# The front of a two-block layer on one core: first weight unit with the first 512 tokens, state-space set-up between low parts, rotations on GpSimd

## The reference

```python
h = rmsnorm(x, g_pre_mix)
proj = jnp.einsum('bld,dn->bln', h, w_in)
(u_s5, x_conv, b_conv, c_conv, q, k, v, f_logit, gate_logits) = jnp.split(proj, offsets, axis=-1)
y_a = s5_mixer(u_s5, a_re, a_im, log_dt, b_re, b_im, c_re, c_im, d_skip, w_glu)
y_b = short_conv_mixer(x_conv, b_conv, c_conv, conv_w)
```

## Time and profile before

| | |
|---|---|
| median of 3 runs | 3327.33 (3326.53 to 3329.29) |
| profiled execution, own time | 3331.32 |
| its span from first to last instruction | 3329.5 |
| mean granted TensorE clock | 0.997 |
| PE busy | 3262.3 (98%) |
| DVE busy | 1937.3 (58%) |
| ACT busy | 1278.2 (38%) |
| POOL busy | 1168.2 (35%) |

### The profile page before, as it was taken

How to read it: one execution, slowest core, us unless ns; L and a number is a source line. 1 busy time by engine, 2 the same in 40 slices (tenths; PEclk the granted TensorE clock), 3 DMA queues, 4 the chain that set the end, 5 groups by cost and what they waited for, 6 DMA issues and landing times.

```text
span 3329.5 us, 41035 instructions
## 1 busy us (share of the span) xinstructions
PE 3262.3 (98%) x16387; PEld 2695.8 (81%) x16387; DVE 1937.3 (58%) x2749; ACT 1278.2 (38%) x2023; POOL 1168.2 (35%) x487
## 2 busy tenths in 40 slices
PE   7899999999999999999999999999999999999998
PEld 6788877888888888788878888888888888888787
DVE  6874446543547766777643344445744376666676
ACT  4223444443136454534533333333332253233433
POOL 2443101444422444455112222222443145455453
PEclk9999999999999999999999999999999999999999
DMA  4233102234533444643421212213335232333553
GB/s 131 64 78 109 32 20 77 101 114 171 180 124 114 164 161 160 213 162 120 139 92 51 63 49 64 63 56 99 111 123 193 98 114 101 114 114 114 196 165 132
DMA packets 242713, 378.75 MB, mean 114 GB/s; under 512 B 22184, under 2 KB 180564, under 8 KB 229852
## 3 DMA queue, kind: packets, MB, share of 16 engines
q1 hardware_dynamic: 212140, 255.58, 24.2%
q10 hardware_dynamic: 26000, 109.81, 8.4%
q0 software_dynamic: 4384, 10.74, 0.9%
HBM read 263.66 MB, written 110.33 MB: 112 GB/s over the span
## 4 chain that ended last, share of the span: by engine, by line
PE 90%; DVE 4%; ACT 2%; DMA 2%; issue 1%; POOL 1%; SPq 0%; ACTq 0%; DVEq 0%; POOLq 0%
PE ps L1327 27%; PE ps L351 17%; PE ps L2201 13%; PE ps L842 5%; PE ps L306 3%; PE ps L1482 2%; PE ps L1484 2%; PE ps L1473 2%; PE ps L327 2%; PE ps L334 2%; PE ps L333 2%; PE ps L3871 2%; PE ps L3842 1%; PE ps L368 1%; PE ps L2243 1%; PE ps L3350 1%
## 5 line engine op out<-in xcount | busy, mean ns | idle before, releaser
L298 POOL TENSOR_TENSOR wlo<-raw,whi 128x2048 fp32r<-128x2048 f32 (+1 forms) x85 | 296.9, 3493 | 874.3 <-ACT whi L290 873.9
L1327 PE MATMUL ps<-h_hi,own 128*128 128x512 f32 x1200 | 385.5, 389 | 0.0
L1327 PE MATMUL ps<-tb,whi 128*128 128x512 f32 x1200 | 369.5, 389 | 0.0
L351 PE MATMUL ps<-h_lo,whi 128*128 128x512 f32 x880 | 352.3, 400 | 4.6 <-POOL wlo L298 4.6
L351 PE MATMUL ps<-h_hi,wlo 128*128 128x512 f32 x880 | 344.8, 392 | 0.0
L997 POOL TENSOR_TENSOR own<-raw,own 128x1024 fp32r<-128x1024 f32 x50 | 139.7, 2794 | 423.8 <-ACT own L987 423.8
L1025 POOL TENSOR_TENSOR wlo<-wsum,whi 128x2048 fp32r<-128x2048 f32 x50 | 239.4, 4788 | 100.5 <-ACT whi L1020 100.5
L1327 PEld LDWEIGHTS ps<-tb,whi 128*128 128x128 f32 x1200 | 225.2, 188 | 47.2 <-POOL wlo L1025 0.4
L1327 PEld LDWEIGHTS ps<-h_hi,own 128*128 128x128 f32 x1200 | 225.3, 188 | 46.5
L2201 PE MATMUL ps<-dw,h_lo 128*128 128x512 f32 x1104 | 253.3, 389 | 0.0
L2201 PEld LDWEIGHTS ps<-dw,h_lo 128*128 128x128 f32 x1104 | 207.3, 188 | 43.0
(11 more groups left out here) (424 smaller groups left out, 7325.8 us busy)
## 6 DMA issues: line engine op xcount, KB each, us to landing
raw<-in_w_in_dram SPq DMA_DIRECT2D x57, 512.0 KB, 4.4
raw<-in_w_in_dram SPq DMA_DIRECT2D x28, 1024.0 KB, 5.3
f_keep<-fr ACTq DMA_DIRECT2D x27, 1024.0 KB, 3.9
raw<-in_w_ff_dram SPq DMA_DIRECT2D x24, 1024.0 KB, 5.7
s_keep<-fr ACTq DMA_DIRECT2D x24, 1024.0 KB, 5.2
xh<-s_keep SPq DMA_DIRECT2D x48, 512.0 KB, 3.7
g_keep<-fr ACTq DMA_DIRECT2D x20, 1024.0 KB, 3.9
fr<-g_keep SPq DMA_DIRECT2D x20, 1024.0 KB, 5.0
```

The source lines that it names most:

```text
L298: nc.gpsimd.tensor_tensor(wlo[c % 2][:, 0:cols], raw[c % 2][:, 0:cols], whi[c % 2][:, 0:cols].bitcast(F32), ALU.subtract).then_inc(s_lo.se ...
L351: x = nc.tensor.matmul(ps[:, bank, :], w(a, k, m * P, P), H[b][:, k, sl], start=j == 0, stop=j == 23)
L1327: last = nc.tensor.matmul(ps[:, bank, :], w[p][:, k, :], x[r][:, k, :], start=k == 0 and q == 0, stop=k == 3 and q == 2)
```

## The change

- `Start`: the x pairs 2 and 3 are issued behind the square of tile 2. ScalarE makes the high part of unit 0 ahead of the h_hi parts, and each tile's square stands behind two h_hi parts. VectorE has `step_argument` ahead of the first h_lo, and the other pieces of the set-up (step size, decay argument, angle, reduction) between the h_lo parts of tokens 512 to 1023; ScalarE has the two tanh and two sine functions there.
- SP: unit 0 waits for x pair 0 instead of 1, unit 1 for x pair 2 instead of unit 0.
- TensorE: only blocks 0 and 1 are turned before the low part of unit 0 is waited for; block k + 2 is turned behind pass k; blocks of tokens 512 to 1023 are turned with unit 1.
- GpSimd: `turns` (45 tensor_tensor ops of 32 columns) and `first_tables` (24 ops of 32 to 256 columns) are new on it and gone from VectorE; VectorE waits for them ahead of `turn_tables(0)`. In group 1 the low part of (1,1) comes ahead of the half tables.
- VectorE, group 0: `first_half` follows `turn_tables`; `inputs` and then both `by_c` follow `powers`.
- TensorE: 14 half tiles instead of 16 lie ahead of the outputs of group 0; of the two others one comes before and one behind `turn_y(0)`.
- ScalarE, group 1: the high part and `x_tile(1,0)` come ahead of gelu.

```diff
@@ Start.act
-                e.wait_ge(x_pair[0].sem, 16)
-                load(2)
-                load(3)
-                for t in range(8):
+                for t in range(4):
                     r.act_pre(e, t)
-                    if t == 3:
-                        e.wait_ge(dv.sem, self.d + 1)
-                    if t == 5:
-                        split_hi(e, unit_no(0))
+                    if t == 2:
+                        load(2)
+                        load(3)
+                e.wait_ge(dv.sem, self.d + 1)
+                split_hi(e, unit_no(0))
+                for t in range(4, 8):
                     if t == 7:
                         split_hi(e, unit_no(1))
-                    if t >= 4:
-                        r.act_hi(e, 0, 2 * t - 8)
-                        r.act_hi(e, 0, 2 * t - 7)
+                    r.act_hi(e, 0, 2 * t - 8)
+                    r.act_hi(e, 0, 2 * t - 7)
+                    r.act_pre(e, t)
+                self.parameters.function(e, 0)
                 for k in range(8):
                     r.act_hi(e, 1, k)
+                    if k == 3:
+                        self.parameters.function(e, 1)
+                for n in (2, 3):
+                    self.parameters.function(e, n)
@@ Start.dve
+                p = self.parameters
+                p.step_argument(e)
+                for t in range(4, 8):
+                    r.dve_lo(e, 0, 2 * t - 8)
+                    r.dve_lo(e, 0, 2 * t - 7)
+                    r.dve_norm(e, t)
                 for k in range(8):
                     r.dve_lo(e, 1, k)
+                    if k == 0:
+                        p.step_size(e)
+                    elif k == 1:
+                        p.decay_argument(e)
+                    elif k == 2:
+                        p.angle(e)
+                    elif k in (3, 4, 5):
+                        p.reduced(e, k - 3)
+                    elif k == 6:
+                        p.angle_argument(e)
@@ S5AndConv.sp
-                e.wait_ge(x_pair[1].sem, 16)
+                e.wait_ge(x_pair[0].sem, 16)
...
                     if j == 0:
-                        e.wait_ge(ld[0].sem, 16)
+                        e.wait_ge(x_pair[2].sem, 16)
@@ S5AndConv.act
                 for f in range(4):
-                    if f:
+                    if f == 1:
+                        split(f, 1)
+                        x_tile(f, 0)
                         gelu(f - 1)
...
@@ S5AndConv.pool
+                def turns():
+
+                    S = [sm[:, j, :] for j in range(20)]
+                    e.wait_ge(m["s5_cos"], 1)
+                    r, i = S[8], S[7]
+                    for k in range(3):
+                        tt(S[18], r, i, ALU.mult)
+                        tt(MR[:, 0, :], r, r, ALU.mult)
+                        tt(MI[:, 0, :], i, i, ALU.mult)
+                        tt(MR[:, 0, :], MR[:, 0, :], MI[:, 0, :], ALU.subtract)
+                        tt(MI[:, 0, :], S[18], S[18], ALU.add)
+                        r, i = MR[:, 0, :], MI[:, 0, :]
+                    for j in range(6):
...
+                def first_tables():
...
+                turns()
                 split(0, 0)
+                first_tables()
                 for f in range(4):
-                    if f < 2:
-                        if f:
-                            half_tables(f)
-                        split(f, 1)
-                    else:
-                        split(f, 1)
+                    split(f, 1)
+                    if f:
                         half_tables(f)
@@ S5AndConv.dve
                     if f == 0:
-                        first_tables()
+                        e.wait_ge(m["s5_turns"], 1)
+                        e.wait_ge(m["s5_first"], 1)
                         turn_tables(f)
-                        by_c(f, 0)
+                        first_half()
                     powers(f)
...
                     else:
+                        inputs(f)
+                        by_c(f, 0)
                         by_c(f, 1)
-                        first_half()
                         taps(f)
                         by_b(f, 0)
                         kernel_rows(f)
                         by_b(f, 1)
-                        inputs(f)
@@ S5AndConv.pe
-                for k in range(KT):
-                    r.turn(e, 0, k)
+                r.turn(e, 0, 0)
+                r.turn(e, 0, 1)
                 lo_w(0)
                 for k in range(KT):
-                    r.turn(e, 1, k)
                     e.wait_ge(lo_made.sem, r.lo + k + 1)
                     u_passes(0, 0, k, 0)
+                    if k + 2 < KT:
+                        r.turn(e, 0, k + 2)
                 lo_w(1)
                 for k in range(KT):
+                    r.turn(e, 1, k)
                     u_passes(1, 0, k, 2)
...
-                    half_tiles((2, 0, 3, 3)[f])
+                    half_tiles((2, 1, 3, 3)[f])
                     if f:
                         turn_y(f - 1)
-                    if f > 1:
+                    if f:
                         half_tiles(1)
...
-                    half_tiles(6 if f else 7)
+                    half_tiles(6 if f else 5)
                     outputs(f)
```

More of the change, by code:

```diff
@@ L670, in hybrid_kernel, with __init__, link, tt @@
         m = {n: x.sem for n, x in m.items()}
+        class Parameters:
+            def __init__(self):
+                self.n = 0
+                self.S = [sm[:, j, :] for j in range(20)]
+            def link(self, e, ins):
+                ins.then_inc(m["s5_step"], 1)
+                self.n += 1
+                e.wait_ge(m["s5_step"], self.n)
+            def tt(self, e, o, a, b, op):
+                self.link(e, nc.vector.tensor_tensor(o, a, b, op))
+            def ts(self, e, o, a, s1, op0, s2=None, op1=ALU.bypass):
+                self.link(e, nc.vector.tensor_scalar(o, a, s1, s2, op0, op1))
+            def function(self, e, n):
+                o, i, fn, sc = ((1, 0, ACT.Tanh, 0.5), (5, 4, ACT.Tanh, 0.5), (7, 6, ACT.Sin, 1.0), (8, 6, ACT.Sin, 0.5))[n]
+                if n != 3:
+                    e.wait_ge(m["s5_arg"], n + 1)
+                nc.scalar.activation(sm[:, o, :], sm[:, i, :], fn, scale=sc).then_inc(m["s5_fun"], 1)
+            def expm1(self, e, o, th):
+                S = self.S
+                self.ts(e, S[10], th, -1.0, ALU.mult, 1.0, ALU.add)
+                self.link(e, nc.vector.reciprocal(S[10], S[10]))
+                self.tt(e, o, th, S[10], ALU.mult)
+                self.ts(e, o, o, 2.0, ALU.mult)
+            def step_argument(self, e):
+                S = self.S
+                e.wait_ge(m["s5_ld"], 16 * 5)
+                e.wait_ge(m["s5_d"], 16)
+                self.ts(e, S[9], S[19], 1.4426950408889634, ALU.mult)
+                self.ts(e, S[9], S[9], MAGIC, ALU.add, -MAGIC, ALU.add)
+                self.ts(e, S[9], S[9], -127.0, ALU.max, 127.0, ALU.min)
+                self.ts(e, S[0], S[9], -LN2_PARTS[0], ALU.mult)
+                self.tt(e, S[0], S[0], S[19], ALU.add)
+                self.ts(e, S[10], S[9], -LN2_PARTS[1], ALU.mult)
+                nc.vector.tensor_tensor(S[0], S[0], S[10], ALU.add).then_inc(m["s5_arg"], 1)
+                self.ts(e, S[9], S[9], 127.0, ALU.add, 8388608.0, ALU.mult)
+                self.link(e, nc.vector.tensor_copy(ki[:, :], S[9]))
+            def step_size(self, e):
+                S = self.S
+                e.wait_ge(m["s5_fun"], 1)
+                self.expm1(e, S[2], S[1])
+            def decay_argument(self, e):
+                S = self.S
+                self.ts(e, S[2], S[2], 1.0, ALU.add)
+                self.tt(e, S[2], S[2], ki[:, :].bitcast(F32), ALU.mult)
+                nc.vector.tensor_tensor(S[4], S[3], S[2], ALU.mult).then_inc(m["s5_arg"], 1)
+            def angle(self, e):
+                S = self.S
+                self.tt(e, S[6], S[11], S[2], ALU.mult)
+                self.ts(e, S[9], S[6], 1.0 / TWO_PI, ALU.mult)
+                self.ts(e, S[9], S[9], MAGIC, ALU.add, -MAGIC, ALU.add)
+            def reduced(self, e, *parts):
+                S = self.S
+                for c in parts:
+                    self.ts(e, S[10], S[9], -PI_PARTS[c], ALU.mult)
+                    self.tt(e, S[6], S[6], S[10], ALU.add)
+            def angle_argument(self, e):
+                S = self.S
+                self.ts(e, S[6], S[6], 3.1415925, ALU.min, -3.1415925, ALU.max)
+                nc.vector.tensor_copy(S[12], S[6]).then_inc(m["s5_arg"], 1)
@@ L2478, in act @@
                             e.wait_ge(d_u[q].sem, 16)
-                    x_tile(f, 0)
+                    if f != 1:
+                        x_tile(f, 0)
                     if f:
@@ L2590, in dve @@
[L2590 to L2600, removed]
@@ L4074, in hybrid_kernel @@
         start = add(Start())
-        mixers = add(S5AndConv(start.rows))
+        mixers = add(S5AndConv(start.rows, start.parameters))
         mixers.decay = add(Decay())
```

118 lines of the change are left out of this document (44 added, 74 removed), and 2 rows, old and new, of the table m.

## The result

The changed kernel took **3335.59 us** (median of 11 runs, 3332.93 to 3338.95), the kernel before 3327.8 beside it on the same chip: ratio 1.0023, interval 1.0016 to 1.0031. It is slower by a little more than the 0.2% that can be told from no change. The forecast was 3326.5 in a range up to 3335: wrong by 9.1 us, and on the side that the sum had left to a rival.

A forecast was written before the change was run, and what follows sets the result against it. TensorE was taken as the bound, with some 11.4 us of waits and 2.4 of slow matmuls to win. Outputs +3.8 and group 1's front -4.6 gave -0.8: 3330.5 profiled, scaled to a 3326.5 median, range 3317 to 3335.

The forecast's parts named there:

- Part 4: GpSimd's turns and first tables: turn ops 0.29 each, 13.1 us in all; tables ready at 91.2, VectorE waits 8.4.
- Part 6: Path to group 0's output products: kernel rows at 125.1, state products 2.7, outputs at 137.6, 3.8 later than before.
- Part 7: Front of group 1: 7.6 us of waits and 2.4 of slow matmuls go, 5.4 of work comes, 4.6 gained.
- Parts 1 to 5: From first weight load to half tile 8: early first pass, late last turn and tables, TensorE standing 6.8 us.
- Part 2: TensorE's passes with turns among them: last turn at 57.2, u products end at 80.4 against 78.26, early start spent.
- Part 1: First weight unit, loaded behind x pair 0: first pass at 24.6, 5.4 us sooner than before.
- Lock per op: Rival: each turn op alternates with a VectorE op, 0.45 apiece; outputs at 146.3, total 3335; chance 0.14.
- Part 4 and 5: GpSimd tables, then VectorE's order behind them: two low parts block 2.2 each, by_c ends at 113.7, TensorE stands 6.8.
- Tables in time: Rival: GpSimd's tables are ready when VectorE finishes WT (82.8); 9.4 us gained, total 3318; chance 0.30.
- The load is no sooner: Rival: first weights share with x pair 1, land near 19, all up to 4 us later; 3330; chance 0.06.

The follow-up runs named there:

- b_group1: Kernel before with only the group 1 edits: half tiles moved, low part of (1,1) ahead of the half tables, x_tile(1,0) ahead of gelu; 3329.82 us, ratio 1.0006.
- o_pool: Changed kernel with only its front undone (weights behind x pair 1, all turns ahead as before); 3324.31 us, ratio 0.9987.
- a_low: Changed kernel, with GpSimd's low part of conv unit (1,1) held back until the states of group 0 are done; 3334.73 us, ratio 1.0021.
- b_front: Kernel before with the new front alone (early weights, turns between passes), set-up and tables left in VectorE's list; 3339.3 us, ratio 1.0032.
- o_tables_low: Changed kernel with the old front, first tables back on VectorE, and low part of (1,1) held until the states are done; 3322.09 us, ratio 0.9982.
- a_tiles: Changed kernel with the half tiles back where they were, GpSimd order kept; 3335.59 us, ratio 1.0021.
- o_low_tiles: o_tables_low with the half tiles also back where they were before the change; 3320.27 us, ratio 0.9975.

## Why the prediction was wrong

**Where it failed.** Three steps: the price of the turn ops in Part 4 (1.4 us by the time the tables are there), the state products of Part 6 (2.0), and the gain of Part 7 (2.6 of 4.6 not there). The last two both belong to the edits at the front of group 1: forecast at 4.6 faster, they came out 1.9 slower (not told apart from no change) when tested alone in b_group1, and that is the larger half of the miss.

**What held.** The mechanism of Parts 1 to 5 is in the trace: the early first pass, the last turn late, the set-up free between low parts, the tables late, VectorE waiting on them, TensorE standing at half tile 8 (5.7 and, new, 2.9 before it, where 6.8 was forecast), two half tiles fewer before the outputs. Part 2 said that the early start is spent, and o_pool against the changed kernel shows it with 11.3 us.

**Part 1 and 2, too late by 2.** The first pass came at 22.4, not 24.6; the last turn ended near 54.8, not 57.2; the u products ended level with before (conv tile read at 83.9 against 84.0), not 2.1 later. It is one error carried through: ScalarE began the high part at 14.16 where the estimate was 15.9. It was on the safe side and should have made the result better.

**Part 4, the first step that failed.** A turn op was priced at 0.29; 38 of the 45 came every 0.33, and the last seven every 0.7 to 0.8, the last lasting 1.3, each held by a VectorE op of 512 or 1024 columns (BA and WT had started, which the step had left out for the turns, though it charged it for the tables). 57.98 to 76.4 is 18.4 us instead of 13.1 to 13.5. That ate the 2.5 which the turns began early and 2.4 more. It is the rival "Lock per op" in part: it decided from 0.43 apiece, and the mean was 18.4 / 45 = 0.41. The low part behind the turns then waited for the VectorE product that had begun 0.18 before it, and took 3.31 where the step had 2.4: it ended at 79.8, forecast 76.4. The tables won 2.0 of this back, 12.8 instead of 14.8, by luck: only the first of their ops was caught (0.98), where the step had charged the first eight with 3.6. So they were there at 92.6, forecast 91.2. The step's own terms are added up 0.8 too high (60.5 + 13.1 is 73.6, not 74.0, and 76.4 + 10.8 + 3.6 is 90.8, not 91.2), which hid as much of the miss.

**Part 4 and 5, a queue not looked at.** The low part of conv unit 1 moved behind the tables on GpSimd. The step charged what it blocks on VectorE (rightly: 4.1 for the two), but not that TensorE waits for it: 2.9 at 95.1, with a slower clock behind it (0.91). It probably cost little of its own, as TensorE stood later for the C product anyway; no run tests that.

**Part 6.** 137.6 was forecast, 141.5 measured. kernel_rows ended at 127.1, not 125.1: 1.4 from the tables, the rest in small pieces behind them. The other 2.0 is the low part of unit (1,1) catching the second state product; the step had VectorE's two state products at 2.7 with gaps, and did not ask what GpSimd, freed of the half tables' wait, would do at that moment. a_low shows this term by itself: 1.9 at the outputs. The path between was not the forecast one either. The last TZ transfer was issued by 132.4 and the slowest took 3.5 to land, so TZ was there by 135.9; VectorE's scans, queued behind `by_b(0,1)`, ran from 131.11 to 136.75, and the state products came behind them. That this stretch took the forecast 9.8 us (127.1 to 136.9) was luck.

**Part 7, the gain that was not there.** 4.6 was forecast; from the outputs to the W copy the changed kernel needs 19.97 where before needed 21.96, so 2.0. The 2.4 of slow matmuls did not go, since the longer stand ahead of the outputs brought the level down there. The step counted the waits and slow matmuls that a move removes, and the work it brings, but not the stand that it leaves where the work came from. b_group1 shows it.

**The sum.** 2.0 + 2.0 of Part 6 and 2.6 of Part 7 are 6.6; with the forecast's -0.8 that gives 5.8 against the 5.6 to 5.7 of the marks. What is left, 2.2 between the marks and the medians and 0.5 between the two medians of before, lies outside what two traces can show. Behind the last mark the profiled execution of before took 3331.32 - 287.19 = 3044.1 and that of after 3043.0, so some of it is the scatter of single executions; the rest was not settled.

**The rivals.** "Tables in time" fell: VectorE waited 11.9, not 0. "The load is no sooner" fell (7.02, and ScalarE had it at 14.16). "Lock per op" gave the right total (3335) by the right lock, though at a few ops and not at all 45, and the state product is of the same kind. The total itself was luck: the rival had the outputs at 146.3 (measured 141.5) and all 4.6 of Part 7. The Trainium skill (SBUF - State Buffer, Who interferes with whom) has the lock held for the whole instruction. The rows agree for long ones: the state product of 1.22 ended 1.09 after the low part that caught it (141.44 against 140.35), so nearly all of its work came behind it.

## What to carry to other kernels

An earlier start of the bounding engine is worth nothing if it puts back the step from which the other engines' lists start: ask first what the last turned block, not the first product, releases. An order of an engine's list can't be judged by itself; the same three moved steps were worth +4 us with VectorE early and -3 with it late, because one step in the list waits for TensorE and another is waited for by it. When work is moved behind a stand, price the stand that it leaves, with the clock behind it.

## What the runs showed of the hardware that was not expected

- GpSimd ops of 32 columns take 0.24 to 0.31 us and come every 0.33 when chained by semaphore; the same ops took 0.63 to 1.32 while VectorE ran ops of 512 and more columns, each ending 0.09 to 0.11 after the VectorE op beside it (75.08 + 1.32 = 76.40 against 75.07 + 1.23 = 76.30).
- The level of TensorE's clock does not follow from the length of one stand alone in these traces. The same stand of 3.76 ahead of the outputs was followed by the full level in the kernel before (a pair of matmuls 0.49) and by the lower one in b_front:

```profile
143.29 0.80 PE L2919 MATMUL ps<-TZ,ug 128*128 128x128 f32 x2 [3.76 <-DVE PP L2777]
```

- It was low also behind stands of 2.9, 3.65 (o_tables_low), 5.7, 9.8 and 11.2, and behind 1.2 and 2.1 in a_tiles; it stayed at full behind the same 1.2 and 2.1 in o_low_tiles, where TensorE had not stood from 80 until the outputs were done. The limit of some 4 us that the expectations of b_group1 and o_low_tiles go by is not borne out.
- The two engines can hold each other up in turn. In the changed kernel the low part began at 76.51, while a VectorE op ran from 76.33 to 77.55, and took 3.31 instead of 2.4; the next VectorE op began at 77.59 and took 3.32 instead of 1.23, ending 1.09 after the low part. So each waited for the one that had begun before it.
